# Modulation blocks of the second mixer: eight column products on TensorE become sums on VectorE

## The reference, cut to what matters

```
mod = silu(c) @ ada_w + ada_b          # [1024] x [1024, 6144]
...
q, k, v = split(h @ w_in, 3)           # h [256, 1024], w_in [1024, 3072]
q, k = rms(q) * q_norm, rms(k) * k_norm
o = softmax(q k^T / sqrt(128) + bias, causal) v
x = x + gate1 * (o @ w_out)
```

## Time and profile before

| what | value |
|---|---|
| median of 3 runs | 2135.22 us (2133.57 to 2136.65) |
| the profiled execution's own time | 2133.7 us |
| its span in the trace | 2131.9 us |
| mean granted TensorE clock | 0.981 |
| TensorE matmul busy | 1936.0 us, 91% |
| VectorE busy | 563.0 us, 26% |
| the mixer of the second layer, first projection to last output product | 726.2 to 880.7 us |

### The profile page before, as it was taken

One profiled execution on the slowest core, in us unless ns is written; L12 is line 12 of the kernel. 1 busy time (PEld: TensorE's weight loads), 2 busy tenths in 40 slices (PEclk: granted clock), 3 DMA queues, 4 the chain that ended last, 5 costly groups with the idle time before them and its releaser, 6 DMA issues. The chain is left out here.

```text
span 2131.9 us, 28620 instructions
## 1 busy us (share of the span) xinstructions
PE 1936.0 (91%) x11309; PEld 992.5 (47%) x11309; DVE 563.0 (26%) x1278; ACT 361.5 (17%) x803; POOL 2.2 (0%) x7
## 2 busy tenths in 40 slices
PE   5896999999988799999999888799999999989986
PEld 1342555544444344555544444354555555544443
DVE  2143622221112323622211122333463311111112
ACT  1141310000000123311000000214322211111111
POOL 0000000000000000000000000000000000000000
PEclk9998999999999899999999999999999999999998
DMA  9846899999999784899999999742327899999995
GB/s 321 309 158 237 358 410 426 425 427 426 426 428 424 277 295 162 353 378 424 425 428 424 427 427 425 234 146 79 119 79 280 363 424 427 425 426 427 425 428 238
DMA packets 130143, 732.34 MB, mean 344 GB/s; under 512 B 18713, under 2 KB 26748, under 8 KB 80790
## 3 DMA queue, kind: packets, MB, share of 16 engines
q1 hardware_dynamic: 130046, 731.29, 84.4%
q10 hardware_dynamic: 24, 0.02, 0.0%
HBM read 730.20 MB, written 4.23 MB: 344 GB/s over the span
## 5 line engine op out<-in xcount | busy, mean ns | idle before, releaser
L276 PE MATMUL psum<-arena,norm_w 128*64 128x256 f32 x6144 | 700.5, 380 | 51.3 <-DMA arena<-in_moe_w_dram 31.4
L276 PEld LDWEIGHTS psum<-arena,norm_w 128*64 128x64 f32 x6144 | 432.1, 136 | 318.3 <-issue 54.9
L307 PE MATMUL psum<-arena,hT 128*64 128x512 f32 x1536 | 349.7, 596 | 33.4 <-DMA arena<-in_moe_w_dram 20.1
L383 DVE TENSOR_TENSOR hT<-psum,arena 64x512 f32<-64x512 f32 x128 | 88.1, 688 | 519.5 <-PE psum L307 518.6
L307 PEld LDWEIGHTS psum<-arena,hT 128*64 128x64 f32 x1536 | 106.8, 136 | 242.8 <-issue 220.2
L466 ACT ACTIVATE hT<-psum 128x256 f32<-128x256 f32 x96 | 36.8, 383 | 1001.6 <-PE psum L276 1001.6
L327 PE MATMUL psum<-hT 128*128 128x512 f32 x384 | 177.6, 605 | 7.7 <-DVE hT L383 6.0
L2189 PE MATMUL psum<-arena,hT 128*128 128x512 f32 (+1 forms) x352 | 153.8, 587 | 2.1 <-PEq L55 1.8
L327 PEld LDWEIGHTS psum<-hT 128*128 128x128 f32 x384 | 69.0, 189 | 97.9 <-issue 85.0
L693 DVE COPY hT<-psum 128x256 f32<-128x256 f32 x96 | 40.8, 425 | 261.9 <-PE psum L295 261.9
L2189 PEld LDWEIGHTS psum<-arena,hT 128*128 128x128 f32 x352 | 65.3, 192 | 70.3 <-issue 68.3
(11 more groups left out here) (399 smaller groups left out, 1234.8 us busy)
## 6 DMA issues: line engine op xcount, KB each, us to landing
arena<-in_moe_w_dram SPq DMA_DIRECT2D x192, 2048.0 KB, 36.6
arena<-in_w_gate_dram SPq DMA_DIRECT2D x32, 2048.0 KB, 33.5
arena<-in_w_up_dram SPq DMA_DIRECT2D x32, 2048.0 KB, 34.8
arena<-in_w_down_dram SPq DMA_DIRECT2D x32, 2048.0 KB, 34.4
arena<-in_ada_w_dram SPq DMA_DIRECT2D x24, 2048.0 KB
arena<-in_w_in_dram SPq DMA_DIRECT2D x10, 2048.0 KB, 7.7
arena<-in_odd_w_in_dram SPq DMA_DIRECT2D x6, 2048.0 KB, 10.2
arena<-in_even_w_in_dram SPq DMA_DIRECT2D x4, 2048.0 KB, 14.9
```

The lines of the kernel that those rows point to most:

```text
L276: m = nc.tensor.matmul(out[64 * half:64 * half + 64, :], xw[:, u, c, :], w[:, c, half * HALF:(half + 1) * HALF], start=(c == 0), stop=(c = ...
L307: m = nc.tensor.matmul(bank_Y[64 * half:64 * half + 64, :], hTs[:, k % 2, (k // 2) * 64:(k // 2) * 64 + 64], experts.slots[slot][2][:, k, ...
L383: return nc.vector.tensor_tensor(y[BLOCK * u:BLOCK * (u + 1), half, :], bank_Y[rows, :], gate2[rows, half * 512:half * 512 + 512], ALU.mult)
```

## The change

The M products go. VectorE makes the sum over the eight chunks itself, in two running sums (`sums`, even and odd chunks), and adds the two into `part`. The bias stands in one partition of a tile of zeroes and starts the even sum. W then is a product with `ones`, which sums over all 128 partitions. The matrix `quads` and the spread copy of c (`crep`) are no longer loaded or made. The slots of ada_w are free when the sum has read them (`mod_used`), not when a TensorE product has. The order of the remaining steps is written anew on all four engines.

```diff
-SIDE_1 = (("P", 0, 0), ("P", 0, 1), ("M", 0), ("P", 1, 0), ("W", 0), ("M", 1), ("P", 1, 1), ("W", 1), ("M", 2), ("P", 2, 0), ("W", 2),
-          ("P", 2, 1), ("M", 3), ("P", 3, 0), ("W", 3), ("P", 3, 1), ("M", 4), ("P", 4, 0), ("W", 4), ("M", 5), ("P", 4, 1), ("W", 5),
-          ("M", 6), ("P", 5, 0), ("W", 6), ("P", 5, 1), ("M", 7), ("W", 7))
+SIDE_1 = (("P", 0, 0), ("P", 0, 1), ("P", 1, 0), ("P", 1, 1), ("W", 0), ("P", 2, 0), ("W", 1), ("P", 2, 1), ("P", 3, 0), ("W", 2),
+          ("P", 3, 1), ("W", 3), ("P", 4, 0), ("P", 4, 1), ("W", 4), ("P", 5, 0), ("W", 5), ("P", 5, 1), ("W", 6), ("W", 7))
...
# SyncE
-            for dst, src in ((quads, w["quads"]), (wq, w["q_norm"].partition_broadcast(P)), (wk, w["k_norm"].partition_broadcast(P))):
+            for dst, src in ((wq, w["q_norm"].partition_broadcast(P)), (wk, w["k_norm"].partition_broadcast(P))):
...
-                if item[0] == "M" and item[1] + 2 < len(mods):
-                    wait_kept(sp, *item)
+                if item[0] == "W" and item[1] + 2 < len(mods):
+                    sp.wait_ge(mod_used, item[1] + 1)
                     load_mod(item[1] + 2)
-            wait_kept(sp, "M", 6)
-            wait_kept(sp, "M", 7)
+            sp.wait_ge(mod_used, len(mods))
             experts.load_router(sp)
...
# TensorE
             def whole(i):
-                wait_kept(pe, "M", i)
+                pe.wait_ge(mod_summed, i + 1)
                 bank_free("W", i)
-                nc.tensor.matmul(side_bank("W", i), quads, part[:, i % 2], start=True, stop=True).then_inc(made[place["W", i] % 2], 1)
+                nc.tensor.matmul(side_bank("W", i), consts["ones"][:, :], part[:, i % 2], start=True, stop=True).then_inc(made[place["W", i] % 2], 1)
...
             project(3, 0)
-            whole(3)
+            whole(2)
...
             score(0)
             project(3, 1)
             score(1)
-            modulate(4)
+            whole(3)
             turn_unit(0)
             project(4, 0)
-            whole(4)
-            modulate(5)
             turn_unit(1)
             project(4, 1)
-            whole(5)
-            modulate(6)
             output_unit(0)
             output_unit(1)
...
             turn_heads(q, 1, 2).then_inc(q_turned, 1)
+            whole(4)
             project(5, 0)
-            whole(6)
+            whole(5)
...
             score(2)
             project(5, 1)
             score(3)
-            modulate(7)
+            whole(6)
             turn_unit(2)
-            whole(7)
...
             output_unit(3)
+            whole(7)
             pe.wait_ge(o_kept, 4)
...
# VectorE
+            def sum_up(i, lo=0, hi=DC):
+                wt = slots[:, i % 2]
+                if lo == 0:
+                    dve.wait_ge(mod_landed[i % 2], 32 * (i // 2 + 1))
+                for c in range(lo, hi):
+                    if c >= 2:
+                        dve.wait_ge(mod_step, (DC + 1) * i + c - 1)
+                    elif i:
+                        dve.wait_ge(mod_step, (DC + 1) * i)
+                    scale_c = ccol[:, c:c + 1]
+                    if c == 1:
+                        r = nc.vector.tensor_scalar(sums[:, 1], wt[:, c], scale_c, None, ALU.mult)
+                    else:
+                        r = nc.vector.scalar_tensor_tensor(sums[:, c % 2], wt[:, c], scale_c, sums[:, c % 2] if c else btile[:, i % 2], ALU.mult, ALU.add)
+                    r.then_inc(mod_step, 1)
+                if hi == DC:
+                    dve.wait_ge(mod_step, (DC + 1) * i + DC)
+                    dve.sem_inc(mod_used, 1)
+                    if i >= 2:
+                        wait_made(dve, "W", i - 2)
+                    nc.vector.tensor_tensor(part[:, i % 2], sums[:, 0], sums[:, 1], ALU.add).then_inc(mod_step, 1)
+                    dve.wait_ge(mod_step, (DC + 1) * (i + 1))
+                    dve.sem_inc(mod_summed, 1)
...
             scale(0)
+            sum_up(3, 0, 4)
             normalise(0)
             scale(1)
-            add_bias(4)
             link(reduce_squares(qT, 1, 1, 6))
             ask(1)
+            sum_up(3, 4, DC)
             normalise(1)
-            add_bias(5)
             norm_heads(1)
-            add_bias(6)
+            sum_up(4, 0, 4)
             keep_output(0)
             keep_output(1)
+            sum_up(4, 4, DC)
+            sum_up(5)
             scale(2)
+            sum_up(6, 0, 4)
             normalise(2)
             scale(3)
-            add_bias(7)
+            sum_up(6, 4, DC)
             normalise(3)
+            sum_up(7, 0, 4)
             keep_output(2)
+            sum_up(7, 4, DC)
             keep_output(3)
```

More of the change, by code:

```diff
@@ L3339, in middle_mixer_stage @@
     ss, rs = arena.take([2, 2, TILES, G]), arena.take([2, 2, TILES, G])
-    wq, wk, crep, quads = arena.take([P]), arena.take([P]), arena.take([DC, 32]), arena.take([P])
+    wq, wk, sums = arena.take([P]), arena.take([P]), arena.take([2, MB])
     assert arena.at <= 20130
@@ L3352, in middle_mixer_stage @@
     made, kept = [sem("made0"), sem("made1")], [sem("kept0"), sem("kept1")]
-    small_landed, zeroed, mod_landed, crep_made = sem("small"), sem("zeroed"), [sem("mod0"), sem("mod1")], sem("crep")
+    small_landed, zeroed, mod_landed, mod_step = sem("small"), sem("zeroed"), [sem("mod0"), sem("mod1")], sem("mod_step")
+    mod_used, mod_summed = sem("mod_used"), sem("mod_summed")
     squared, root_asked, root_done, k_ready, q_ready, k_turned, q_turned, k_copied, q_copied = (
@@ L3502, in _ @@
             project(0, 1)
-            pe.wait_ge(crep_made, 1)
-            modulate(0)
             project(1, 0)
-            pe.wait_ge(small_landed, 48)
+            project(1, 1)
             whole(0)
-            modulate(1)
-            project(1, 1)
+            project(2, 0)
             whole(1)
-            modulate(2)
-            project(2, 0)
-            whole(2)
             project(2, 1)
-            modulate(3)
             pe.wait_ge(k_ready, 1)
@@ L3564, in _ @@
                     out(t, c, 0 if t else G, DC)
-            wait_kept(pe, "M", 7)
+            wait_kept(pe, "P", 5, 1)
             wait_kept(pe, "W", 7)
@@ L3624, in _ @@
             keep(1, 0)
-            finish(0)
             keep(1, 1)
@@ L3628, in _ @@
                 square(q, qT, 1, t, 0)
-            finish(1)
+            finish(0)
             root(0)
             keep(2, 0)
-            finish(2)
+            finish(1)
             keep(2, 1)
@@ L3637, in _ @@
             keep(3, 0)
-            finish(3)
+            finish(2)
             soften(0)
@@ L3642, in _ @@
                 square(q, qT, 3, t, 1)
+            soften(1)
+            finish(3)
             keep_turned(0)
-            soften(1)
             root(1)
             keep(4, 0)
-            finish(4)
             keep_turned(1)
             keep(4, 1)
+            keep_heads(1, 2)
+            finish(4)
+            keep(5, 0)
             finish(5)
-            keep_heads(1, 2)
-            keep(5, 0)
-            finish(6)
             soften(2)
             keep(5, 1)
+            soften(3)
+            finish(6)
             keep_turned(2)
-            soften(3)
+            keep_turned(3)
             finish(7)
-            keep_turned(3)
             serve_scalar(act)
@@ L3731, in keep_output @@
                                       banks[6 + u % 2].rearrange("p (i n) -> p i n", i=G)).then_inc(o_kept, 1)
-            nc.vector.tensor_copy(crep, ccol.unsqueeze(2).to_broadcast([P, DC, 32])).then_inc(crep_made, 1)
-            dve.wait_ge(small_landed, 48)
+            dve.wait_ge(small_landed, 32)
             link(nc.vector.tensor_tensor(wk, wk, wq, ALU.mult))
-            add_bias(0)
+            dve.wait_ge(zeroed, 1)
+            sum_up(0)
             reduce_squares(kT, 0, 0, 0)
-            add_bias(1)
+            sum_up(1, 0, 4)
             link(reduce_squares(qT, 1, 0, 2))
             ask(0)
-            add_bias(2)
+            sum_up(1, 4, DC)
             norm_heads(0)
-            add_bias(3)
+            sum_up(2)
             reduce_squares(kT, 0, 1, 4)
```

## The result

The changed kernel takes 2142.98 us in the median of seven runs (2137.02 to 2148.1), against 2135.22 before (2133.5 to 2136.65 in as many). The ratio is 1.0039, with a 95% interval of 1.0022 to 1.0055: slower, by 7.8 us in the medians. The forecast was 2140.2, in a range of 2134 to 2145. A second set of eleven runs gave 2141.02 against 2134.63, a ratio of 1.0027 (1.0018 to 1.0036), 6.4 us.

The account below looks back on a forecast made before the run. The prediction took TensorE's queue to bound the mixer: -16.7 us removed, +17.9 of waits and +3.8 of clock loss give +5.0 us. From 2133.7 that is 2138.7, with 1.5 to the median 2140.2 us, range 2134 to 2145.

Parts of the forecast that it names:

- TensorE's queue is the bound: In the mixer TensorE is busy 132.29 of 133.80 us, so each microsecond removed or waited counts one for one.
- the mixer's end arrives whole: The experts' transfers are released by TensorE's progress, so a shift of the mixer's end reaches the program's end in full.
- -16.7 us removed: In the mixer, eight M products save 14.9 us and two idle stretches of TensorE 1.8 us.
- A chunk of 0.75 us every 0.66: On VectorE each multiply-add takes 0.75 us, neighbours overlapping by 0.09; half sum 3.7 us, whole sum 6.1.
- Four waits of 7.9, 0.85, 2.85 and 6.3 us: TensorE's added waits at W3, output_unit(0), W4 and W6, together +17.9 us; the other W products have room.
- The clock, +3.8: TensorE's clock falls to 1.2 GHz after the waits at W3 and W6, costing 1.9 us each.
- I leave it at nothing: No clock loss counted for the 2.85 us wait at W4; 1.9 us kept for the range.
- sum of +5.0: Total change: -16.7 us removed, +17.9 us of waits and +3.8 us of clock loss.
- The experts' loads are hidden: First w1 load goes out near 861 + 5 instead of 851.21, still with over 10 us of room before the first expert.
- Median 2140.2: Whole-program time: profiled 2133.7 us plus 5.0 is 2138.7, plus 1.5 for the median of the runs; chance 0.52.

Follow-up runs that it names:

- waits filled: Changed kernel with eight unused TensorE products added ahead of W3 and six ahead of W6; 2134.39 us, ratio 1.0000 to the kernel before.
- shorter half sums: Changed kernel with chunks 4 to 7 of each block summed over only 64 of 512 columns; 2137.28 us, ratio 1.0014 to the kernel before.
- three early sums: Changed kernel with VectorE's second halves of sums 3, 4 and 6 moved ahead of scale(1), keep_output(0) and scale(3); 2118.40 us, ratio 0.9923 to before.
- sum 3 early: Changed kernel with VectorE's second half of sum 3 moved ahead of scale(1); 2132.18 us, ratio 0.9987 to the kernel before.
- W3 later: Changed kernel with TensorE taking W3 after turn_unit(0) and project(4, 0), VectorE's order kept; 2133.24 us, ratio 0.9994 to the kernel before.
- second pair of profiles: Changed kernel and kernel before, each profiled again with no edit; mixer 138.2 against 133.5 us, changed kernel's second set 2141.02 us, ratio 1.0027.

## Why the prediction was right, point by point

- *TensorE's queue is the bound, and the mixer's end arrives whole.* Right where it was tried cleanly: with the waits taken away 16.1 us of mixer became 16.2 of the median. In the other kernels the median moved, against the kernel before, by 2 us less (waits filled) to nearly 4 us more (shorter half sums) than the mixer, so for small changes it holds only within that.
- *-16.7 us removed.* Right: with three early sums the mixer lost 16.1 us, 0.77 of waiting at `output_unit(0)` and 0.6 at `output_unit(2)` still in it.
- *A chunk of 0.75 us every 0.66; a half sum of 3.7, a whole one of 6.1.* Measured 0.746 us a step and 2.74 for four, which is 0.66 apart; from 799.85 to the end of the addition at 803.42 the half sum takes 3.6, and the whole sum 5 takes 6.0. The flush that the Trainium skill has after every operation (VectorE: DVE Perf Modes, section Terms) doesn't show in the spacing of independent neighbours here either. VectorE came to 75 us, forecast 78.
- *Four waits of 7.9, 0.85, 2.85 and 6.3 us.* Measured 7.75, 0.77, 2.58 and 6.12, together 17.2 against 17.9. The others (W0 to W2, W5, W7) waited for nothing, as forecast.
- *The clock, +3.8.* This term was mis-sized. The step that failed is "I leave it at nothing" for the wait at W4. An idle time of 2.58 us brought a fall there in four of the five profiles that have it: the first of the changed kernel (P50 took 8.72 us instead of 7.03, so 1.7 us), sum 3 early, waits filled and W3 later; in the changed kernel's second profile it brought none. Behind W6 the loss was 2.9 us, not 1.9: W6 0.9, `turn_unit` 0.4 and `out` 1.5, from start to start, against the kernel with filled waits. Behind W3 it was 1.4, in W3 and `turn_unit(0)`; P40, forecast near 9 us, took 7.13 (7.65 in the second profile). That is 6.0 in place of 3.8 in the first profile. Against it, this execution reached full clock earlier at the mixer's start: four projections took 28.9 us there, and 16.4 + 2 x 7.0 before, so 1.4 us less. The mixer's +5.1 so agrees with the sum of +5.0 in part by luck; the sum's two errors, -0.7 in the waits and +2.2 in the clock, nearly meet what the start gave back. The second pair of profiles needs no luck: the clock cost 4.2 us there (1.9 behind W3, none behind W4, 2.3 behind W6), the two starts were equal within 0.1 us, and -16.7 + 17.2 + 4.2 = +4.7 us is what the mixer grew by.
- *The experts' loads are hidden.* Right: the first w1 went out at 869.97, and the distance from the last `out` group to the first expert product was 45.8 us, against 46.8 before.
- *Median 2140.2.* Measured 2143.0 and 2141.0, inside the range. The mixer gives about 5 of the 6.4 to 7.8 us and the stretch up to the first expert gives 1.0 back. The rest is in no term of the sum. In the second pair of profiles the 6.2 us between the two executions are 0.1 ahead of the mixer, 4.7 in it, -1.4 from its end to the third layer, 1.1 in the third layer's mixer and 1.7 in the experts behind it, the stretch at the lower clock near the end. In the first pair 5.8 lie ahead and 4.2 in the third layer's mixer. What decides where the clock falls in these unchanged stages wasn't tried, so a remainder of some 3 to 4 us in the medians stays open. Single executions scatter by as much: the changed kernel's over 11 us in the first set and 8 in the second, those of before over 3 and 9.

## What to carry to other kernels

Work moved to an engine that is idle for most of a stage was free here only where it stood in that engine's queue before the instruction that waits for the other engine, not after it, or where the consumer's engine had ready work to take first. Compare, for each product that consumes a result, where the producer's queue is when the consumer arrives; an average of 54% busy says nothing. And count a wait of TensorE with the lower clock behind it: the waits of 4.25 to 7.75 us here brought 1.4 to 2.9 us of it each, and those of 1.88 and 2.58 us 1.6 to 1.7 each time that the clock fell. Here the edit's saving of 16.7 us turned into a loss of 5 by the order of three half sums.

## What the hardware showed unexpectedly

- The clock fell at idle times as short as 2.58 and 1.88 us, inside a stage in which TensorE was busy on both sides of them, though at 2.58 not every time. In the third layer's experts the same 32 records behind an idle time of 2.01 us took 5.36 instead of 3.67 us in two of twelve profiles, and near the end the 16 behind 1.02 us took 5.35 instead of 3.65 in five of twelve. At the waits of 0.71 to 0.97 us in the mixer it didn't fall. So the length of an idle time alone doesn't tell whether the clock falls.
- Filling a wait with products that nobody reads made the kernel 6.6 us faster in the median, 2.8 to 3.6 of it in the mixer, though no real work moved.
- Later stages of unchanged code aren't of constant length. The stretch from the norm stage of the third layer to that layer's first expert product took 304.7 to 312.4 us over the twelve profiles. From there to the end of the span it was 461.1 to 461.4 us in seven of them and 462.8 to 463.1 in the five with the stretch at the lower clock near the end.
